# Between two transformer blocks: one pass over the residual for two norms, and the context normalised by token

## Chip, cores and metric

One Trainium2 chip, one core of it. The metric is the device time of one execution in microseconds (us), the median of several runs. All data are float32. Five engines work side by side: TensorE (PE in the profile; its weight loads are PEld), VectorE (DVE), ScalarE (ACT), GpSimd (POOL) and SyncE (SP), and 16 DMA engines move the data.

## What is computed

Two transformer blocks on 256 tokens of width 1024, one after the other. The first ends in a mixture of experts and a final norm, the second begins with a norm of its own and with a context of 256 more tokens. Cut to what lies between the blocks:

```python
# end of the first block
x = x + g2 * hier_moe(h, ...)                 # 32 experts, 2 for each token
x = rms_norm(x, final_g)
# start of the second block
h     = rmsnorm(x,   g_pre_mix) * (1 + sc1)      + sh1
h_ctx = rmsnorm(ctx, g_pre_mix) * (1 + mod_c[1]) + mod_c[0]
# ... then h @ w_in and h_ctx @ w_in[:, :KV_COLS], attention, merge,
x = x + gt1 * rmsnorm(y, g_post_mix)          # the residual x is used again
# ... then a second mixture of 32 experts, 4 for each token
```

`rms_norm(x, g)` is `x * rsqrt(mean(x*x) + 1e-6) * g`, the mean over the 1024 features.

## The kernel before

Activations lie transposed, features on the partitions: `xT` (the residual) and `hT` (the normalised input) hold 8 slices `k` of 128 features. `xT[:, k, :]` is 256 tokens wide. `hT[:, k, 0:T]` holds the tokens of `x` and `hT[:, k, T:2*T]` those of the context. A per-feature factor is thus one number for each partition, a per-token factor a row of 256 that is the same on all partitions. `hN` is a buffer with tokens on the partitions, and `mgd` is another view of the same memory. `gain[:, j, :]` holds products of gains, `mod2` the second block's shifts and scales, `cols` the gain vectors (`cols[:, 0, 64:72]` is `final_g`).

A norm goes so. ACT squares all 8 slices in one instruction (`square`, L1351). PE sums the squares over the features by 8 products with a matrix of ones (`sumsq`). DVE scales the sum and adds epsilon (`rms`, L1733), ACT takes the root (`sqrt`, L1348), DVE the reciprocal (L1735). DVE then multiplies each slice by gain and row (`modulate`, L1741) and, where there is a shift, adds it in a second loop (L1745). Each step waits for the one before by a semaphore; `mark` and `nth` count them.

Between the blocks three norms stand one after another: `fin` (the final norm, in place on `xT`), `n2` (the second block's norm of it, into `hT[:, :, 0:T]`) and `ctx` (the context's, into `hT[:, :, T:2*T]`). The context is fetched into `hN` by a DMA that POOL issues once the residual of the first block is made ("moe1 out"). PE transposes it in 16 blocks, ACT copies it out of PSUM and squares it. Only when all of "h2" and "hctx" is there does PE begin the projections (`fill2`).

Before that come the experts of the first block (`moe(1)`): 8 groups of 4 experts, whose weights (three chunks of 4 MB for a group) stream through a ring of 12 slots of 1 MB that SP fills. A slot is loaded again when PE has used it. Each engine walks its own program of this loop. The projections of the second block take their weights from the same ring, as do, later, the 32 experts of the second block (12 MB each).

POOL also fetches the attention biases (32 small DMAs, L548), the first 16 right behind the context. DVE, after the norms, normalises and rotates the heads that the first four fills give ("rope") and adds a mask to the biases (`bias(0)`, L1899).

Of the kernel before, what the change touches and what calls it, by code (L numbers as in the profile page):

```python
# [15 lines left out]
ALU = mybir.AluOpType  # L16
# [3 lines left out]
P = 128  # L20
# [119 lines left out]
class Counts:  # L140
# [13 lines left out]
    def nth(self, sem, key):  # L154

        return 1 if self.known is None else self.known[self.names[id(sem)], key]

def program(nc, A, const, ssm, tables, out, known):
# [3 lines left out]
    with ExitStack() as ctx:  # L163
# [104 lines left out]
        PT = [LA(1024), LA(1024)]  # L268
        sgl = LA(2, 2, T)
        mgd = hN[:, :, :].rearrange("p a b -> p (a b)").rearrange("p (k t) -> p k t", t=T)  # L270
        yS = LA(4, T)
        oT = LA(KD, T)
        stat = sb("stat", [P, 2, 16])
# [251 lines left out]
        def _(g):  # L525
# [8 lines left out]
                                                   cols[:, 0, 72 + 16 * kv + c:73 + 16 * kv + c], None, ALU.add)  # L534
                last.then_inc(blocks_made, 1)

            g.wait_ge(madeV, nth(madeV, "moe1 out"))
            g.dma_start(hN[:, :, :], A["ctx_2"].rearrange("(a p) d -> p a d", p=P)).then_inc(ctx_in, 16)

            for tt in range(TT):  # L540
                if tt == 1:
                    g.wait_ge(filled, nth(filled, ("S", 2, 3)))
                for h in range(8):
                    for r in range(2):
                        row = 2 * tt + r
                        src = bass.AP(tensor=A["rpb_2"].tensor, offset=h * 465 + (7 - row) * 31 + 15 - 63,
                                      ap=[[1, 64], [31, 4], [1, 64]])
                        g.dma_start(nab2[64 * r:64 * r + 64, h, :].rearrange("p (a b) -> p a b", b=64), src).then_inc(bias_in[tt], 16)  # L548
# [12 lines left out]
        def _(pe):  # L561
# [6 lines left out]
            def transpose(dst, src):  # L568
                return nc.tensor.transpose(dst, src, ident[0:src.shape[0], 0:src.shape[0]])  # L569
# [636 lines left out]

            last = mm(ps[:, 0, 0:1], ones, csil[:, 0:1], start=True, stop=True)
            last.then_inc(filled, mark(filled, "moe1"))
            sumsq("fin", 0, hT[:, :, T:2 * T])

            sumsq("n2", 0, hT[:, :, T:2 * T])
            pe.wait_ge(ctx_in, 16)
            for tt in range(TT):
                for k in range(KD):
                    last = transpose(ps[:, 1 + tt * 2 + k // 4, (k % 4) * P:(k % 4 + 1) * P], hN[:, tt, k * P:(k + 1) * P])
            last.then_inc(filled, mark(filled, "ctx"))
            pe.wait_ge(madeA, nth(madeA, ("sq", "ctx")))
            for k in range(KD):
                last = mm(ps[:, 5, 0:T], ones, mgd[:, k, :], start=k == 0, stop=k == KD - 1)
            last.then_inc(filled, mark(filled, ("ss", "ctx")))  # L1220
            pe.wait_ge(madeV, nth(madeV, "h2"))
            pe.wait_ge(madeV, nth(madeV, "hctx"))

            turn2 = [0]

# [7 lines left out]
            def fill2(outs):  # L1233

                b, g = bank2()
                for o, lhs, rhs in outs:
                    for k in range(KD):
                        last = mm(o(b), lhs(k), rhs(k), start=k == 0, stop=k == KD - 1)
                last.then_inc(filled, mark(filled, ("p2", g)))

# [96 lines left out]
        def _(act_):  # L1337
# [309 lines left out]
            sigmoids("gates")  # L1647
            moe_front(1)
            moe(1)
            act_.wait_ge(madeV, nth(madeV, "moe1 out"))  # L1650
            square("fin", xT[:, :, :])
            sqrt("fin", rstd[:, 0:T])
            act_.wait_ge(madeV, nth(madeV, "x2"))
            square("n2", xT[:, :, :])
            sqrt("n2", rstd[:, 0:T])
            act_.wait_ge(filled, nth(filled, "ctx"))
            for tt in range(TT):
                for q in range(2):
                    last = copy(hT[:, 4 * q:4 * q + 4, T + tt * P:T + (tt + 1) * P], ps[:, 1 + tt * 2 + q, :].rearrange("p (k t) -> p k t", t=P))
            act_.drain()  # L1660
            a(mgd, hT[:, :, T:2 * T], ACT.Square).then_inc(madeA, mark(madeA, ("sq", "ctx")))
            sqrt("ctx", rstd[:, T:2 * T])
            turn2 = [0]

            def take2(fn):
# [53 lines left out]
        def _(v):  # L1719
# [43 lines left out]
            def step(ins):  # L1763
                v.drain()
# [192 lines left out]
            tt_(gain[:, 0, :], mod2[:, 40:48, 0], cols[:, 1, 72:80], ALU.mult)  # L1957
            v.drain()
            tt_(wr1, wr1, B(gain[:, 1, :], 36), ALU.mult)
            merge("branch", "gates", "mgd")  # L1960
            clear_tables(1)
            for c in range(4):
# [213 lines left out]

            moe_front(1)
            moe(1)
            v.wait_ge(filled, nth(filled, "moe1"))
            for k in range(KD):  # L2180
                last = stt(xT[:, k, :], ps[:, 4 + k // 2, (k % 2) * T:(k % 2 + 1) * T], mod1[:, 40 + k:41 + k], xT[:, k, :], ALU.mult, ALU.add)
            last.then_inc(madeV, mark(madeV, "moe1 out"))
            rms("fin", 0, rstd[:, 0:T])
            modulate(xT[:, :, :], xT[:, :, :], rstd[:, 0:T], cols[:, 0, 64:72], None, "x2")

            V.memset(crow[:, 3, 2:3], 0.0).then_inc(madeV, mark(madeV, ("shift", 2)))
            rms("n2", 0, rstd[:, 0:T])
            modulate(hT[:, :, 0:T], xT[:, :, :], rstd[:, 0:T], gain[:, 2, :], mod2[:, 0:8, 0], "h2")
            rms("ctx", 5, rstd[:, T:2 * T])
            modulate(hT[:, :, T:2 * T], hT[:, :, T:2 * T], rstd[:, T:2 * T], gain[:, 3, :], mod2[:, 0:8, 1], "hctx")  # L2190

            v.wait_ge(emptied, nth(emptied, ("p2", 3)))
            q3 = lambda x: x.rearrange("p t (h d) -> p (t h) d", d=HD)
# [91 lines left out]
```

## Time and profile before

| what | us |
| --- | --- |
| median of 3 runs | 2142.71 |
| lowest and highest run | 2140.18, 2146.76 |
| the profiled execution | 2141.7 |
| its span, first to last instruction | 2139.9 |
| PE busy in it | 1885.5 (88%) |
| DVE, ACT, POOL busy | 538.6, 385.6, 44.5 |
| mean granted PE clock | 0.947 |
| mean DMA rate | 293 GB/s |

### The profile page before, as it was taken

The numbers are of one execution on the slowest core, as the hardware profiler recorded it, in microseconds if no ns is written. First come the engines' busy times: TensorE is split into PE (matmuls) and PEld (weight loads), VectorE is DVE, ScalarE is ACT, GpSimd is POOL, SyncE is SP. The second block draws the span as 40 slices with busy tenths as digits, with TensorE's granted clock in tenths as the row PEclk, the third lists the DMA queues.
The fourth block names the chain that finished last, engine by engine and source line by source line (L and its number), as shares of the span: only waits on it lengthen the run. The fifth ranks groups of instructions, "written<-read, shape, count | busy, mean of one in ns | idle before, by whom it ended". The sixth has DMA issues, their size and how long they took to land.

```text
span 2139.9 us, 28358 instructions
## 1 busy us (share of the span) xinstructions
PE 1885.5 (88%) x10935; PEld 1070.9 (50%) x10938; DVE 538.6 (25%) x1231; ACT 385.6 (18%) x875; POOL 44.5 (2%) x107
## 2 busy tenths in 40 slices
PE   6999999976686779999988999888998999988895
PEld 4664678854444466677753443333333344333333
DVE  3675332121111223232421111111111111111112
ACT  3232452021110110243120111111110111110012
POOL 0030000000000200100000000000000000000000
PEclk9999899988888889899978999999998999999998
DMA  9969622319999712233342999999999599999993
GB/s 399 370 232 358 240 79 88 149 36 417 418 418 387 272 43 79 67 92 102 142 169 112 416 418 417 416 416 418 417 417 401 241 417 418 416 417 417 418 417 152
DMA packets 108344, 626.77 MB, mean 293 GB/s; under 512 B 11168, under 2 KB 15264, under 8 KB 49792
## 3 DMA queue, kind: packets, MB, share of 16 engines
q1 hardware_dynamic: 106112, 618.81, 71.5%
q0 software_dynamic: 1584, 4.33, 1.1%
q10 hardware_dynamic: 560, 2.35, 0.3%
q8 instruction: 70, 1.15, 0.2%
q14 instruction: 18, 0.15, 0.0%
HBM read 624.39 MB, written 1.05 MB: 292 GB/s over the span
## 4 chain that ended last, share of the span: by engine, by line
PE 59%; DMA 21%; SPq 11%; issue 3%; DVE 3%; ACT 2%; DVEq 0%; ACTq 0%
PE ps L452 56%; DMA ring<-in_w_gu_dram 14%; SPq L501 6%; SPq L504 5%; DMA ring<-in_moe_w_gate_dram 4%; PE ps L569 3%; DMA ring<-in_ada_w_dram 1%; ACT arena L1344 1%; DMA ring<-in_moe_w_down_dram 1%; DMA ring<-in_w_mod_dram 1%; SPq L474 0%; DVE rstd L1735 0%; DVE arena L2099 0%; PE ps L815 0%; SPq L411 0%
## 5 line engine op out<-in xcount | busy, mean ns | idle before, releaser
L452 PE MATMUL ps<-ring,arena 128*64 128x512 f32 (+2 forms) x5248 | 918.4, 564 | 126.7 <-issue 54.5
L452 PEld LDWEIGHTS ps<-ring,arena 128*64 128x64 f32 (+1 forms) x5248 | 293.5, 131 | 692.2 <-issue 501.5
L452 PE MATMUL ps<-arena 64*128 64x256 f32 (+10 forms) x1762 | 263.0, 378 | 31.9 <-ACT arena L1344 15.9
L452 PE MATMUL ps<-hT,ring 128*128 128x256 f32 (+1 forms) x960 | 237.0, 402 | 2.3 <-DVE hT L1781 2.3
L452 PEld LDWEIGHTS ps<-arena 64*128 64x128 f32 (+6 forms) x1764 | 155.6, 164 | 136.4 <-issue 76.4
L452 PEld LDWEIGHTS ps<-hT,ring 128*128 128x128 f32 x960 | 180.3, 192 | 58.8 <-issue 33.7
L2125 DVE TENSOR_SCALAR arena<-ps 128x512 f32<-128x512 f32 x34 | 23.5, 692 | 549.9 <-PE ps L452 549.9
L1344 ACT ACTIVATE arena<-ps 128x256 f32<-128x256 f32 (+4 forms) x195 | 107.3, 574 | 291.3 <-PE ps L452 150.3
L1608 ACT ACTIVATE arena<-ps,mod,gain 128x128 f32<-128x128 f32 x180 | 67.7, 458 | 435.2 <-PE ps L452 435.2
L452 PE MATMUL ps<-arena,hN 128*128 128x128 f32 (+1 forms) x960 | 129.0, 294 | 15.4 <-DVE arena L2075 9.0
L452 PEld LDWEIGHTS ps<-arena,hN 128*128 128x128 f32 x960 | 120.0, 205 | 40.8 <-issue 16.7
L1619 ACT ACTIVATE arena<-arena 128x512 f32<-128x512 f32 (+1 forms) x44 | 25.7, 584 | 615.9 <-DVE arena L2125 417.1
L452 PE MATMUL ps<-ring,hT 128*128 128x256 f32 (+2 forms) x416 | 82.7, 377 | 8.4 <-DVE hT L1745 8.4
L569 PE MATMUL ps<-consts,arena 128*128 128x128 f32 x526 | 75.0, 280 | 11.3 <-DVE arena L2131 8.2
L452 PEld LDWEIGHTS ps<-ring,hT 128*128 128x128 f32 (+1 forms) x416 | 70.1, 186 | 21.6 <-DVE hT L1745 8.8
L2113 DVE COPY arena<-ps 128x512 f32<-128x512 f32 x34 | 23.5, 692 | 220.0 <-PE ps L452 220.0
L452 PE MATMUL ps<-arena,ring 128*128 128x256 f32 x352 | 76.5, 380 | 0.7 <-ACT arena L1344 0.7
L569 PEld LDWEIGHTS ps<-consts,arena 128*128 128x128 f32 x526 | 61.4, 143 | 28.9 <-DVE arena L2131 10.5
L452 PEld LDWEIGHTS ps<-arena,ring 128*128 128x128 f32 x352 | 66.7, 190 | 10.3 <-ACT arena L1344 0.9
L1517 ACT ACTIVATE arena<-ps,stat 128x15 f32<-128x15 f32 (+3 forms) x128 | 56.1, 448 | 80.8 <-DVE stat L1877 80.8
L1877 DVE TENSOR_REDUCE stat<-ps 128x2 f32<-128x1024 f32 (+3 forms) x40 | 36.7, 917 | 131.2 <-PE ps L452 131.2
L452 PE MATMUL ps<-hN,ring 128*128 128x256 f32 x256 | 56.4, 380 | 0.0
(257 smaller groups left out, 920.1 us busy)
## 6 DMA issues: line engine op xcount, KB each, us to landing
ring<-in_w_gu_dram SPq DMA_DIRECT2D x256, 1024.0 KB, 20.0
ring<-in_w_dn_dram SPq DMA_DIRECT2D x128, 1024.0 KB, 23.3
ring<-dense_dram SPq DMA_DIRECT2D x56, 1024.0 KB, 10.6
ring<-in_moe_w_gate_dram SPq DMA_DIRECT2D x32, 1024.0 KB, 12.7
ring<-in_moe_w_up_dram SPq DMA_DIRECT2D x32, 1024.0 KB, 19.1
ring<-in_moe_w_down_dram SPq DMA_DIRECT2D x32, 1024.0 KB, 18.1
ring<-in_ada_w_dram SPq DMA_DIRECT2D x24, 1024.0 KB, 18.3
ring<-in_w_mod_dram SPq DMA_DIRECT2D x24, 1024.0 KB, 8.6
```

The lines of the kernel that those rows point to most:

```text
L452: ins = nc.tensor.matmul(*a, start=start, stop=stop, **k)
L501: sp.dma_start(ring[:, i % RING, :], src).then_inc(full[i % RING], 16)
L504: sp.dma_start(slot_ap(i, (2, D)), src).then_inc(full[i % RING], 16)
L569: return nc.tensor.transpose(dst, src, ident[0:src.shape[0], 0:src.shape[0]])
L1344: return a(dst, src, ACT.Copy, scale=scale)
L1517: last = a(e_[:, s * nk:s * nk + m], ps[:, bank, at:at + m], ACT.Exp, bias=stat[:, i % 2, s:s + 1], accum_out=stat[:, i % 2, 4 + s:5 + s])
L1608: last = a(dst[:, d, :], ps[:, bank, k * P:(k + 1) * P], ACT.Identity, scale=gs[:, d:d + 1], bias=sh[:, d:d + 1])
L1619: a(sg[:, 0:w], glu[:, 0:w], ACT.Sigmoid, scale=1.702 if n == 2 else 1.0).then_inc(s["sig"], 1)
L1877: V.tensor_reduce(dst, sc[:, :, :, 0:m], AX.X, ALU.max, negate=True).then_inc(madeV, mark(madeV, ("mx", n, i)))
L2113: V.tensor_copy(dst, ps[:, 3, :]).then_inc(s["ys"], 1)
L2125: ts(glu, ps[:, 1, :], 7.0, None, ALU.min).then_inc(s["glu"], 1)
```

## The change

- The residual is made in four chunks of two slices ("moe1 out", c). For each chunk ACT writes two sets of squares: of `x` into `mgd` and of `x * final_g` into `o2`. PE sums both, into two banks.
- The two norms are merged. With s1 = mean(x*x) and s2 = mean((x*final_g)^2), DVE forms s2 + eps*(s1 + eps). One over its root is the product of both norms' rows. `gain[:, 2, :]` gets `final_g` as a further factor, and `hT[:, :, 0:T]` is made from `xT` directly. DVE multiplies, ACT adds the shift, chunk by chunk, and the first fill waits for each chunk as it comes to it.
- The residual itself is scaled by `final_g` and its own row afterwards.
- The context is fetched after "router" of the first block, into `ctxN`, a view of memory in `hT` that is free then. Its statistics are taken with tokens on the partitions, by ACT with `accum_out`, in ACT's program behind its loop of the experts. PE transposes the rows already scaled (`context_turn`), and ACT applies gain and shift as it copies them out of PSUM (`context_out`). PE no longer sums squares of the context.
- POOL's first 16 bias DMAs wait for "moe1" instead of "moe1 out".

```diff
+        hflat = hT[:, :, :].rearrange("p a b -> p (a b)")
+        ctxN = hflat[:, 0:TT * D].rearrange("p (a b) -> p a b", b=D)
 # POOL
-            g.wait_ge(madeV, nth(madeV, "moe1 out"))
-            g.dma_start(hN[:, :, :], A["ctx_2"].rearrange("(a p) d -> p a d", p=P)).then_inc(ctx_in, 16)
+            g.wait_ge(filled, nth(filled, ("router", 1)))
+            g.dma_start(ctxN, A["ctx_2"].rearrange("(a p) d -> p a d", p=P)).then_inc(ctx_in, 16)
+            g.wait_ge(filled, nth(filled, "moe1"))
 # PE
-            sumsq("fin", 0, hT[:, :, T:2 * T])
-            sumsq("n2", 0, hT[:, :, T:2 * T])
-            pe.wait_ge(ctx_in, 16)
-            for tt in range(TT):
+            def context_turn(tt, bank):
                 for k in range(KD):
-                    last = transpose(ps[:, 1 + tt * 2 + k // 4, (k % 4) * P:(k % 4 + 1) * P], hN[:, tt, k * P:(k + 1) * P])
-            last.then_inc(filled, mark(filled, "ctx"))
-            pe.wait_ge(madeA, nth(madeA, ("sq", "ctx")))
-            for k in range(KD):
-                last = mm(ps[:, 5, 0:T], ones, mgd[:, k, :], start=k == 0, stop=k == KD - 1)
-            last.then_inc(filled, mark(filled, ("ss", "ctx")))
-            pe.wait_ge(madeV, nth(madeV, "h2"))
-            pe.wait_ge(madeV, nth(madeV, "hctx"))
+                    last = transpose(ps[:, bank + k // 4, (k % 4) * P:(k % 4 + 1) * P], ctxN[:, tt, k * P:(k + 1) * P])
+                last.then_inc(filled, mark(filled, ("ctx", tt)))
+            pe.wait_ge(madeA, nth(madeA, "ctx rows"))
+            context_turn(0, 2)
+            for c in range(4):
+                pe.wait_ge(madeA, nth(madeA, ("sq", "fin", c)))
+                for k in (2 * c, 2 * c + 1):
+                    for n, sq in enumerate((mgd, o2)):
+                        last = mm(ps[:, n, 0:T], ones, sq[:, k, :], start=k == 0, stop=k == KD - 1)
+                if c == 1:
+                    context_turn(1, 4)
+            last.then_inc(filled, mark(filled, ("ss", "fin")))
 # PE, fill2
+                if g == 1:
+                    pe.wait_ge(madeA, nth(madeA, "hctx"))
                 for o, lhs, rhs in outs:
                     for k in range(KD):
+                        if g == 0 and k % 2 == 0:
+                            pe.wait_ge(madeA, nth(madeA, ("h2", k // 2)))
 # ACT
-            square("fin", xT[:, :, :])
+            act_.wait_ge(ctx_in, 16)
+            for tt in range(TT):
+                a(hflat[:, (2 + tt) * D:(3 + tt) * D], ctxN[:, tt, :], ACT.Square, accum_out=rn[:, tt:tt + 1])
+            act_.drain()
+            a(rn[:, 4:6], rn[:, 0:2], ACT.Sqrt, scale=1.0 / D, bias=rn[:, 2:3]).then_inc(madeA, mark(madeA, "ctx std"))
+            act_.wait_ge(madeV, nth(madeV, "ctx r"))
+            for tt in range(TT):
+                last = a(ctxN[:, tt, :], ctxN[:, tt, :], ACT.Identity, scale=rn[:, 4 + tt:5 + tt])
+            last.then_inc(madeA, mark(madeA, "ctx rows"))
+            for c in range(4):
+                act_.wait_ge(madeV, nth(madeV, ("moe1 out", c)))
+                a(mgd[:, 2 * c:2 * c + 2, :], xT[:, 2 * c:2 * c + 2, :], ACT.Square)
+                for k in (2 * c, 2 * c + 1):
+                    last = a(o2[:, k, :], xT[:, k, :], ACT.Square, scale=cols[:, 0, 64 + k:65 + k])
+                last.then_inc(madeA, mark(madeA, ("sq", "fin", c)))
+            def context_out(tt, bank, ks):
+                for k in ks:
+                    last = a(hT[:, k, T + tt * P:T + (tt + 1) * P], ps[:, bank + k // 4, (k % 4) * P:(k % 4 + 1) * P], ACT.Identity,
+                             scale=gain[:, 3, k:k + 1], bias=mod2[:, k, 1:2])
+                return last
+            act_.wait_ge(filled, nth(filled, ("ctx", 0)))
+            context_out(0, 2, (0, 1, 4, 5, 6, 7))
             sqrt("fin", rstd[:, 0:T])
-            act_.wait_ge(madeV, nth(madeV, "x2"))
-            square("n2", xT[:, :, :])
-            sqrt("n2", rstd[:, 0:T])
-            act_.wait_ge(filled, nth(filled, "ctx"))
-            for tt in range(TT):
-                for q in range(2):
-                    last = copy(hT[:, 4 * q:4 * q + 4, T + tt * P:T + (tt + 1) * P], ps[:, 1 + tt * 2 + q, :].rearrange("p (k t) -> p k t", t=P))
-            act_.drain()
-            a(mgd, hT[:, :, T:2 * T], ACT.Square).then_inc(madeA, mark(madeA, ("sq", "ctx")))
-            sqrt("ctx", rstd[:, T:2 * T])
+            act_.wait_ge(filled, nth(filled, ("ctx", 1)))
+            context_out(0, 2, (2, 3))
+            context_out(1, 4, range(KD)).then_inc(madeA, mark(madeA, "hctx"))
+            for c in range(4):
+                act_.wait_ge(madeV, nth(madeV, ("h2 scaled", c)))
+                for k in (2 * c, 2 * c + 1):
+                    last = a(hT[:, k, 0:T], hT[:, k, 0:T], ACT.Identity, bias=mod2[:, k, 0:1])
+                last.then_inc(madeA, mark(madeA, ("h2", c)))
+            sqrt("x2", rstd[:, T:2 * T])
 # DVE, with the other gains of the first block
+            tt_(gain[:, 2, :], gain[:, 2, :], cols[:, 0, 64:72], ALU.mult)
+            V.memset(rn[:, 2:3], EPS)
 # DVE, between the blocks
+            v.wait_ge(madeA, nth(madeA, "ctx std"))
+            V.reciprocal(rn[:, 4:6], rn[:, 4:6]).then_inc(madeV, mark(madeV, "ctx r"))
             v.wait_ge(filled, nth(filled, "moe1"))
+            for c in range(4):
+                for k in (2 * c, 2 * c + 1):
+                    last = stt(xT[:, k, :], ps[:, 4 + k // 2, (k % 2) * T:(k % 2 + 1) * T], mod1[:, 40 + k:41 + k], xT[:, k, :], ALU.mult, ALU.add)
+                last.then_inc(madeV, mark(madeV, ("moe1 out", c)))
+            V.memset(crow[:, 3, 2:3], 0.0).then_inc(madeV, mark(madeV, ("shift", 2)))
+            v.wait_ge(filled, nth(filled, ("ss", "fin")))
+            r12, r1 = rstd[:, 0:T], rstd[:, T:2 * T]
+            step(ts(r12, ps[:, 0, 0:T], EPS / D, EPS * EPS, ALU.mult, ALU.add))
+            stt(r12, ps[:, 1, 0:T], 1.0 / D, r12, ALU.mult, ALU.add).then_inc(madeV, mark(madeV, ("var", "fin")))
+            ts(r1, ps[:, 0, 0:T], 1.0 / D, EPS, ALU.mult, ALU.add).then_inc(madeV, mark(madeV, ("var", "x2")))
+            v.wait_ge(madeA, nth(madeA, ("std", "fin")))
+            step(V.reciprocal(r12, r12))
+            for c in range(4):
+                for k in (2 * c, 2 * c + 1):
+                    last = stt(hT[:, k, 0:T], xT[:, k, :], gain[:, 2, k:k + 1], r12, ALU.mult, ALU.mult)
+                last.then_inc(madeV, mark(madeV, ("h2 scaled", c)))
+            v.wait_ge(madeA, nth(madeA, ("std", "x2")))
+            step(V.reciprocal(r1, r1))
             for k in range(KD):
-                last = stt(xT[:, k, :], ps[:, 4 + k // 2, (k % 2) * T:(k % 2 + 1) * T], mod1[:, 40 + k:41 + k], xT[:, k, :], ALU.mult, ALU.add)
-            last.then_inc(madeV, mark(madeV, "moe1 out"))
-            rms("fin", 0, rstd[:, 0:T])
-            modulate(xT[:, :, :], xT[:, :, :], rstd[:, 0:T], cols[:, 0, 64:72], None, "x2")
-            V.memset(crow[:, 3, 2:3], 0.0).then_inc(madeV, mark(madeV, ("shift", 2)))
-            rms("n2", 0, rstd[:, 0:T])
-            modulate(hT[:, :, 0:T], xT[:, :, :], rstd[:, 0:T], gain[:, 2, :], mod2[:, 0:8, 0], "h2")
-            rms("ctx", 5, rstd[:, T:2 * T])
-            modulate(hT[:, :, T:2 * T], hT[:, :, T:2 * T], rstd[:, T:2 * T], gain[:, 3, :], mod2[:, 0:8, 1], "hctx")
+                stt(xT[:, k, :], xT[:, k, :], cols[:, 0, 64 + k:65 + k], r1, ALU.mult, ALU.mult)
```

## Rows read from the trace of the kernel before

**Rows 1.** The page, part 4: the chain that ended last, by engine.
```profile
PE 59%; DMA 21%; SPq 11%; issue 3%; DVE 3%; ACT 2%; DVEq 0%; ACTq 0%
```
**Rows 2.** The chain in order of time: start us, us, what.
```profile
725.38 0.69 DVE arena L2111
...
774.93 98.28 PE ps L452 x384
...
1290.96 25.20 DMA ring<-in_w_gu_dram
```
**Rows 3.** Timeline between the blocks: start, us, engine, line, what [idle before <-releaser].
```profile
718.67 0.67 ACT L1344 ACTIVATE arena<-ps 128x256 f32<-128x256 f32 x2
...
726.12 3.72 PE L452 MATMUL ps<-arena 128*128 128x256 f32 x16 [1.41 <-DVE arena L2111]
...
729.99 3.23 DVE L2181 SCALAR_TENSOR_TENSOR xT<-ps,mod,xT 128x256 f32<-128x256 f32 x8 [3.93 <-PE ps L452]
...
735.18 1.28 ACT L1348 ACT_TABLE_LOAD   x1
...
735.21 6.28 PE L452 MATMUL ps<-hT,consts 128*128 128x256 f32 x16 [5.26 <-ACT hT L1351]
741.53 0.43 DVE L1733 TENSOR_SCALAR rstd<-ps 128x256 f32<-128x256 f32 x1 [8.31 <-PE ps L452]
741.99 0.42 ACT L1348 ACTIVATE rstd<-rstd 128x256 f32<-128x256 f32 x1 [5.53 <-DVE rstd L1733]
742.44 1.75 DVE L1735 RECIPROCAL rstd<-rstd 128x256 f32<-128x256 f32 x1 [0.48 <-ACT rstd L1348]
744.27 3.26 DVE L1741 SCALAR_TENSOR_TENSOR xT<-xT,cols,rstd 128x256 f32<-128x256 f32 x8
...
755.32 1.91 PE L569 MATMUL ps<-consts,hN 128*128 128x128 f32 x16
...
772.64 2.19 DVE L1745 TENSOR_SCALAR hT<-hT,mod 128x256 f32<-128x256 f32 x8
```
**Rows 4.** Windows of 2 us: stretch, busy us by engine, PEclk, DMA share, GB/s.
```profile
730.00:732.00 2.00, 0.00 (x0) 0.00 (x0) 2.00 (x6) 0.00 (x0) 0.00 (x0) 1.00 0.98 406
732.00:734.00 2.00, 0.00 (x0) 0.00 (x0) 1.22 (x4) 0.75 (x1) 0.47 (x1) 0.90 1.05 438
734.00:736.00 2.00, 0.79 (x2) 0.70 (x3) 0.00 (x0) 1.98 (x2) 2.00 (x4) 0.50 1.00 414
...
756.00:758.00 2.00, 1.23 (x12) 0.99 (x10) 1.57 (x1) 1.13 (x3) 0.00 (x0) 1.00 0.00 0
...
774.00:776.00 2.00, 1.07 (x3) 0.92 (x4) 0.83 (x4) 0.00 (x0) 0.00 (x0) 0.50 0.00 0
```
**Rows 5.** Windows during the first experts, same columns.
```profile
440.00:460.00 20.00, 12.38 (x152) 10.53 (x156) 5.40 (x19) 4.89 (x9) 0.00 (x0) 0.83 0.01 2
...
520.00:560.00 40.00, 24.35 (x256) 15.04 (x260) 5.02 (x12) 2.47 (x7) 0.00 (x0) 0.79 1.01 417
```
**Rows 6.** ACT by form, whole span: busy us, mean ns of one, idle before.
```profile
L1608 ACT ACTIVATE arena<-ps,mod,gain 128x128 f32<-128x128 f32 x180 | 67.7, 458 | 435.2 <-PE ps L452 435.2
...
L1517 ACT ACTIVATION_READ_ACCUMULATOR arena<-ps,stat 128x1 f32 x128 | 25.7, 201 | 0.0
L1344 ACT ACTIVATE arena<-ps 128x1024 f32<-128x1024 f32 x24 | 24.6, 1025 | 29.6 <-PE ps L569 29.5
...
L1583 ACT ACTIVATE hT<-xT 128x512 f32<-128x512 f32 x8 | 5.0, 630 | 72.4 <-DVE xT L1966 66.8 <-DVE xT L2244 5.6
...
L1700 ACT ACTIVATE arena<-ps,gain 128x256 f32<-128x256 f32 x8 | 3.4, 470 | 48.3 <-PE ps L452 48.3
```
**Rows 7.** Timeline of the projections: head rotation on DVE, end of the fills.
```profile
808.84 2.29 DVE L1899 TENSOR_TENSOR arena<-arena,consts 128x2048 f32<-128x2048 f32 x1
...
821.85 0.29 DVE L2219 COPY arena<-arena 128x256 f32<-128x256 f32 x1
...
873.04 1.91 PE L569 MATMUL ps<-consts,arena 128*128 128x128 f32 x16
```

More of the change, by code:

```diff
@@ L1649, in _ @@
             moe(1)
-            act_.wait_ge(madeV, nth(madeV, "moe1 out"))
-            square("fin", xT[:, :, :])
-            sqrt("fin", rstd[:, 0:T])
-            act_.wait_ge(madeV, nth(madeV, "x2"))
-            square("n2", xT[:, :, :])
-            sqrt("n2", rstd[:, 0:T])
-            act_.wait_ge(filled, nth(filled, "ctx"))
-            for tt in range(TT):
-                for q in range(2):
-                    last = copy(hT[:, 4 * q:4 * q + 4, T + tt * P:T + (tt + 1) * P], ps[:, 1 + tt * 2 + q, :].rearrange("p (k t) -> p k t", t=P))
```

## The prediction, made before the changed kernel was run

> **What bounds the kernel now.** First I read the page's chain: 59% of it is PE, 21% DMA, and DVE and ACT together only 5% [rows 1]. So work on DVE or ACT counts only where PE stands and waits for it. Then the chain in order of time around the change: the last copy of the experts' output on DVE at 725.38, and one unbroken piece of 98.28 us of PE from 774.93, the projections [rows 2]. The timeline between these two shows what lies there. DVE makes the residual from 729.99 [rows 3]. From then to 774.93 the engines hand one another a chain with nothing beside it: squares, sums, root, reciprocal, multiply, three times over. That is 44.9 us, of which PE needs little. All of it is on the path that sets the end, and this is the stretch the change rebuilds.
>
> Behind it the chain is PE up to the second experts and then DMA [rows 2]. Their weights stream through a ring whose slots PE frees, so an earlier start of PE is an earlier start of everything. I count a microsecond won at 774.93 as a microsecond at the end.
>
> **Part 1, the context's load.** It moves to the point where the first block's router is done. In a window soon after it the DMA engines are busy 0.01 of the time, while they are full at 417 GB/s from 520 on [rows 5]. If the 1 MB lands in the idle stretch it costs nothing; if it falls entirely into the full one it costs 1.05 MB / 417 GB/s = 2.5 us. The idle stretch is nearer: I take 0. POOL issues nothing else in between, so the new wait holds back only its bias loads, which come some microseconds earlier than before.
>
> **Part 2, the context's rows.** They lie in ACT's program behind its loop, so they run at the tail of the last group and not during the first experts. ACT's last copy there ends at 719.34 (718.67 + 0.67 [rows 3]). Then come two squares of 1024 elements with a sum each, at 1.03 + 0.20 us [rows 6] = 2.5; the table load that stood at 735.18, 1.28 us [rows 3]; and a small root, 0.3. With half a microsecond to leave the loop that ends at about 723.9. DVE is busy with the last copy until 726.07 (725.38 + 0.69 [rows 2]), so it does the reciprocal at once, and ACT scales the rows, 2 x 1.1 us, to 728.6. PE's sums of the experts' output run to about 729.9 [rows 3]. The cover is 1.3 us. Without it, whatever ACT is late delays PE's first transposes and ACT's first squares; all of Part 2 uncovered would be 6.5 us.
>
> **Part 3, the sums.** DVE makes the residual in 3.23 us, 0.81 for a chunk of two slices [rows 3]: chunk 0 at 730.9, the others at 731.6, 732.4, 733.2. ACT needs for each chunk a square of 512 elements and two of 256 with a scale from memory. The first I take at 0.57, a bit under the mean of 0.63 for one, since neighbours overlap; the second is 3.4 / 8 = 0.42 [rows 6]. That is 1.43 for a chunk, so ACT gives chunk 0 at 732.4 and chunk 3 at 736.6. PE needs four products of 256 columns for a chunk. The scatter just before gives 3.72 / 8 = 0.465 us for one at full clock; the sums of the old norm took 6.28 / 8 = 0.785 [rows 3], for which the clock was at 0.50 when they began [rows 4]. I take full clock: PE is busy to 729.9 in both kernels, the new sums begin 2.5 us later, and in the old kernel the clock still read 1.00 and 0.90 in the windows from 730 to 734 with PE idle [rows 4]. So each chunk is 1.86 us and PE, not ACT, sets the pace. Four chunks are 7.4 us, and the second half of the context's transposes stands among them, 8 x 0.12 = 1.0 us by the 1.91 us for sixteen [rows 3]. The sums end at 732.4 + 8.4 = 740.8.
>
> Here a rule speaks against the full clock. The Trainium skill ("TensorE: Matmul & The Clock Gate", Part 4: PE-mode transpose) says that transposes do not count as activity for the clock in the way products do. The eight transposes at about 730 would then keep nothing awake, and those in the middle would be a gap. The trace does not bear it out plainly: in the window from 756 to 758, which holds the end of the sixteen transposes, the clock was 1.00 [rows 4]. By the rule taken strictly the sums would run as in the second rival below.
>
> **Part 4, from the sums to PE.** DVE forms the variance in two dependent steps of 0.43 [rows 3], with a drain 1.0 us: 741.8. ACT's root is 0.42: 742.3. DVE's reciprocal is 1.75, its first chunk 0.82 (3.26 for eight [rows 3]): 744.9. ACT meanwhile has ten pieces of the context to write out, each of 128 elements with scale and bias from memory. One alone is 0.46 [rows 6], in a row I take 0.38, so 3.8 us: 746.1. The first six were done while PE summed. Then ACT adds the shift to chunk 0, 2 x 0.42: PE starts at 747.0. So ACT, not DVE, is late here, by 1.2 us. Later chunks come every 0.85 us. PE begins at half clock, as it did at 774 [rows 4], and needs 1.57 us for two slices, so it doesn't wait for them. The context is complete before fill 1 wants it. At 0.46 for each piece, and 0.53 for each add, the start would be 748.0.
>
> On this the Trainium skill ("ScalarE: Activation LUTs", Rules for kernel authors) says that adds and multiplies belong on VectorE. The trace agrees: DVE's shift is 2.19 / 8 = 0.27 us [rows 3] against 0.42 here. By the rule the two adds would follow DVE's own multiply and PE would start at about 745.6; as built, 747.0.
>
> **What is removed** is the rest: two of the three roots and reciprocals on the path, the second and third sum, and 16 multiplies and 16 adds in whole loops. None of it needs a price of its own, because I compare start with start: 774.93 - 747.0 = 27.9 us.
>
> **Part 5, what moves behind.** The residual's own reciprocal and eight multiplies (1.75 + 3.26 [rows 3]) now follow on DVE, beside the first fills. DVE then finds fills 0 to 3 to rotate. That work ended at 822.14 while PE came for it at 873.04 [rows 7]: 51 us of cover, of which nothing is used, as both move. The biases were in by 808.84 [rows 7]; they are wanted 28 us earlier now and issued 4 us earlier. They share that cover. The one more gain on DVE lies before the first experts, where it waits for PE: 0 to 0.2 us. Extra waits in the first fill: 0 to 0.5 us.
>
> **The sum.** The profiled execution took 2141.7 us (its span 2139.9 and 1.8 around it); 2141.7 - 27.9 + 0.3 = 2114.1. It lay 1.0 below the median of the runs shown, so against that I expect 2115; I predict 2114.5.
>
> **Rivals.**
> First, a late ACT. Its program behind the loop starts late, or its pieces don't overlap. For it: three of my prices are from rows of other shapes, and the cover in Part 2 is 1.3 us. Against: before, ACT had nothing to do from 719.34 until the residual was made [rows 3]. Price 1 to 6.5 us: 2115.5 to 2121, middle 2118.
> Second, sums at half clock. Sixteen products at 0.785 are 12.6 us instead of 7.4, and the transposes 2.0 instead of 1.0: + 6.2, so 2120.7. For it: PE does only 1 us of transposes between 729.9 and 732.4. Against: [rows 4] as above.
> Third, the gain is given back before the end: the biases or the rotation turn up late for the attention. It would need more than the 51 us of cover to be gone. That would be no change, 2142. I see no mechanism in the rows.
> Fourth, on the other side: slower. The new first fill begins with a wait at each of its pairs of slices. If this keeps the clock at 0.50 in the projections, their 98.28 us [rows 2], nearly all at full clock, would double at worst: 2114 + 90 = 2204. It decides from 34 us more, about a third of the projections at half clock. Against: chunks come at 0.85 us and PE uses 1.57 for each at half clock, so it has no gaps.
>
> **How the numbers follow.** The forecast, 2110 to 2117, gets 0.62. A late ACT gets 0.20, half clock 0.11, the third 0.02, the fourth 0.02, and 0.03 is for a gain over 32 us, if ACT's pieces are cheaper and the chain shorter than priced. From the forecast's lower end to the half-clock case with the load's 2.5 us is 2109 to 2123, about 0.9; I keep it, since the bounds ask for it. Less than 0.3% (6.4 us) is about what a measurement of this kernel can't tell from no change. Faster by more: 0.95; within: 0.03; slower: 0.02.
>
> **What would show it.** In the profile after: ACT's squares of the rows ended before 724 and its scaled rows before 730; PE's sums with "ones" from 732.4 to 740.8 in about 7.4 us busy at a clock of 1.00; ACT's context pieces between 742.3 and 746; the first product of hT at 747, and the same 98 us behind it; no new wait of PE up to the first scores. The prediction is wrong if the projections start after 751, if the stretch up to 726 grows because the load met the experts' weights, or if what was won at 747 isn't there at the end.

## The result, and the profile after

The changed kernel takes 2108.26 us (median of 4 runs, 2107.66 to 2109.01), the kernel before in the same comparison 2141.44. The ratio is 0.9844, with a 95% interval of 0.9831 to 0.9858: 33.2 us less. I had predicted 2114.5 with a range of 2109 to 2123, so the sign and the mechanism held and the gain was larger than the range allowed. The measured median lies 0.7 us below the range.

The timeline of the changed kernel between the blocks, start, us, engine, line, what:

```profile
716.85 0.67 ACT L1353 ACTIVATE arena<-ps 128x256 f32<-128x256 f32 x2
...
719.64 1.28 ACT L1663 ACT_TABLE_LOAD   x1
...
720.94 0.30 ACT L1663 ACTIVATE rn<-rn 128x2 f32<-128x2 f32 x1
...
724.35 2.19 ACT L1666 ACTIVATE hT<-hT,rn 128x1024 f32<-128x1024 f32 x2 [3.12 <-DVE rn L2213]
...
728.17 3.23 DVE L2217 SCALAR_TENSOR_TENSOR xT<-ps,mod,xT 128x256 f32<-128x256 f32 x8 [3.86 <-PE ps L454]
...
729.09 0.63 ACT L1670 ACTIVATE hN<-xT 128x512 f32<-128x512 f32 x1 [2.54 <-DVE xT L2217]
...
730.56 0.70 PE L454 MATMUL ps<-hN,consts 128*128 128x256 f32 x2 [1.50 <-ACT arena L1672]
...
734.12 1.04 PE L572 MATMUL ps<-consts,hT 128*128 128x128 f32 x8
...
738.02 0.59 PE L454 MATMUL ps<-arena,consts 128*128 128x256 f32 x2
738.65 0.42 DVE L2223 TENSOR_SCALAR rstd<-ps 128x256 f32<-128x256 f32 x1 [7.24 <-PE ps L454]
...
739.62 0.42 ACT L1357 ACTIVATE rstd<-rstd 128x256 f32<-128x256 f32 x1 [3.08 <-DVE rstd L2224]
739.94 3.59 ACT L1678 ACTIVATE hT<-ps,mod,gain 128x128 f32<-128x128 f32 x10
740.07 1.75 DVE L2227 RECIPROCAL rstd<-rstd 128x256 f32<-128x256 f32 x1 [0.15 <-ACT rstd L1357]
741.89 3.25 DVE L2230 SCALAR_TENSOR_TENSOR hT<-xT,gain,rstd 128x256 f32<-128x256 f32 x8
743.37 3.32 ACT L1691 ACTIVATE hT<-hT,mod 128x256 f32<-128x256 f32 x8
...
744.46 30.04 PE L454 MATMUL ps<-ring,hT 128*128 128x256 f32 x128 [5.85 <-ACT hT L1691]
```

Read it against [rows 3]. From the start of the residual to the first projection there were 44.94 us, now there are 16.29 (744.46 - 728.17). The context's root was done at 721.24, and its scaled rows at 726.54, before PE had summed the experts' output. PE's sums, with the transposes among them, run without a gap from 730.56 to 738.61. ACT's ten pieces of the context end at 743.53, and the first shift waits for them: DVE's first chunk was ready at 742.77.

The windows show the clock. A row has the stretch, its length, the busy times of PE, PEld, DVE, ACT and POOL, and then the granted share, here 1.00, 1.00, 0.80 and 0.50:

```profile
730.00:734.00 4.00, 3.44 (x16) 3.05 (x17) 1.41 (x5) 4.00 (x11) 4.00 (x8) 1.00 1.05 312
734.00:738.60 4.60, 4.60 (x26) 3.77 (x24) 0.00 (x0) 2.54 (x8) 4.26 (x7) 1.00 1.03 224
738.60:744.40 5.80, 0.01 (x1) 0.00 (x0) 5.44 (x11) 4.78 (x14) 0.00 (x0) 0.80 0.99 266
744.40:748.00 3.60, 3.54 (x8) 2.87 (x9) 1.72 (x3) 2.60 (x7) 0.00 (x0) 0.50 0.93 248
```

The sums ran at 1.00 throughout. The clock fell while PE stood for 5.8 us, and the projections began at 0.50.

To see where the 33 us come from I cut four profiles at the same five events: two executions of the kernel before and two of the changed one. The events are the start of the residual (R), the first projection (F), the first scores of the second block's attention (S), the merge behind the attention (M, a piece of 57.26 us on the chain), and the second experts in their steady pace (B, the piece of 20.2 us). The last column is the span of the profile. Worked out from timeline and chain:

| us | to R | R to F | F to S | S to M | M to B | B to end | span |
| --- | --- | --- | --- | --- | --- | --- | --- |
| before | 729.99 | 44.94 | 102.48 | 125.51 | 164.32 | 972.7 | 2139.9 |
| before, second profile | 730.97 | 45.01 | 102.49 | 125.52 | 164.33 | 972.6 | 2140.9 |
| changed | 728.17 | 16.29 | 103.16 | 123.20 | 162.71 | 973.7 | 2107.2 |
| changed, second profile | 729.40 | 16.28 | 102.95 | 123.18 | 159.46 | 973.5 | 2104.8 |
| mean difference | -1.7 | -28.7 | +0.6 | -2.3 | -3.2 | +1.0 | -34.4 |

The stretch that I costed gives 28.7. The rest, 5.7 us in these profiles, is spread over places that the change doesn't touch. The experiments ask whether it depends on when the projections start, on one part of the change, or on something else.

### The profile page after: what moved, and what is told of

Its sections match the earlier page's. It is cut to its first block, busy times and chain, and to the rows that moved or that the text cites. A ratio compares the mean times of both kernels' runs of the same rounds, so it can differ in the third digit from the quotient of the medians.

```text
span 2107.2 us, 28339 instructions
## 1 busy us (share of the span) xinstructions
PE 1873.6 (89%) x10921; PEld 1062.7 (50%) x10922; DVE 528.8 (25%) x1209; ACT 396.0 (19%) x910; POOL 44.4 (2%) x107
## 4 chain that ended last, share of the span: by engine, by line
PE 59%; DMA 22%; SPq 11%; issue 3%; DVE 2%; ACT 2%; DVEq 1%; ACTq 0%
PE ps L454 57%; DMA ring<-in_w_gu_dram 14%; SPq L503 5%; SPq L506 5%; DMA ring<-in_moe_w_gate_dram 4%; PE ps L572 3%; DMA ring<-in_ada_w_dram 1%; ACT arena L1353 1%; DMA ring<-in_moe_w_down_dram 1%; DMA ring<-in_w_mod_dram 1%; SPq L476 0%; DVE arena L2132 0%; PE ps L818 0%; DVEq L1795 0%; ACT arena L1617 0%
```

## The experiments

Each kernel is the changed one with a small edit, unless it says otherwise. Ratios are to the kernel before on the same chip, with their 95% interval.

**1. A delay put back.** Seventeen idle reciprocals on DVE give the projections nearly their old place.

```diff
+            for n in range(17):
+                V.reciprocal(mgd[:, n % 8, :], cst("time", 1, T + 1))
+                if n % 8 == 7:
+                    v.drain()
             step(V.reciprocal(r12, r12))
```

> The changed kernel with 17 reciprocals of 256 elements on DVE put ahead of its own (they write to memory that nobody reads; the output is unchanged). They delay the first projection by 17 x 1.75 less the 0.6 us by which ACT was later than DVE, 29.3 us, which puts it 45.6 us behind the residual where the kernel before had 44.9. Theory 'one for one': only the start of the projections counts, and the 4.5 us that the change won beyond its stretch of 28.7 us are scatter or lie elsewhere in the change; then 2108.3 + 29.3 = 2137.6, ratio to before 0.998. Rival 'everything hangs on the start' (a later start also lands later pieces worse, so all of the 33.2 goes): 2142, ratio 1.000. Rival 'absorbed': under 2130.

Measured: 2136.17 us, ratio 0.9981 (0.9972 to 0.9989). R to F is 43.50 (729.35 to 772.85), 27.2 more than in the changed kernel, and the total is 27.9 more than 2108.3. One for one holds within the noise: the two kernels ran in different comparisons, and by their ratios to the kernel before the difference is 29 us. The rival that ties everything to the start falls: with a stretch only 1.5 us shorter than before, the kernel is still 3.8 us faster than the 2140.0 measured beside it.

**2. The norms alone.** The context goes the old way; its sums stand between the first and the second fill.

```diff
-            g.wait_ge(filled, nth(filled, ("router", 1)))
-            g.dma_start(ctxN, ...)
+            g.wait_ge(madeV, nth(madeV, ("moe1 out", 3)))
+            g.dma_start(hN[:, :, :], ...)
 ...
                 if g == 1:
-                    pe.wait_ge(madeA, nth(madeA, "hctx"))
+                    pe.wait_ge(madeA, nth(madeA, ("sq", "ctx")))
+                    for k in range(KD):
+                        last = mm(ps[:, 6, 0:T], ones, mgd[:, k, :], start=k == 0, stop=k == KD - 1)
+                    last.then_inc(filled, mark(filled, ("ss", "ctx")))
+                    pe.wait_ge(madeV, nth(madeV, "hctx"))
```

> The merged, chunked norms alone; the context is loaded when the residual is made and goes the old way (turned, copied, squared, summed, scaled on DVE), its sums between the first and the second fill. PE waits for the load before its transposes, until about 746 instead of 744.5, starts fill 0 at 749, then stands before fill 1 for squares, sums and scaling of the context until about 768 where the changed kernel was there at 752. One for one: 2108.3 + 16.6 = 2125, ratio 0.992. Rival: the context's part hides beside fill 0 and the norms alone give nearly all: 2112, ratio 0.986.

Measured: 2127.46 us, ratio 0.9940 (0.9927 to 0.9953). The timeline has the waits that were expected, first for the load and then for the scaled context:

```profile
746.96 3.67 PE L571 MATMUL ps<-consts,hN 128*128 128x128 f32 x16 [5.47 <-DMA hN<-in_ctx_dram]
750.43 7.33 PE L454 MATMUL ps<-ring,hT 128*128 128x256 f32 x32
757.59 3.62 PE L454 MATMUL ps<-hN,consts 128*128 128x256 f32 x16
769.56 20.77 PE L454 MATMUL ps<-ring,hT 128*128 128x256 f32 x83 [8.35 <-DVE hT L1768]
```

The norms alone leave the context's chain bare. It hid nothing but its load beside them. The total is 2.5 us above the 2125 expected, and the chain of this run has an idle time of PE of 2.33 us before the second experts, which the changed kernel lacks (experiment 6).

**3. The context's part alone.** The norms run one after another as before, with their squares in `mgd`. The edit is shown against the kernel before.

```diff
+            sumsq("fin", 0, mgd)
+            context_turn(1, 4)
+            sumsq("n2", 0, mgd)
+            pe.wait_ge(madeV, nth(madeV, "h2"))
+            pe.wait_ge(madeA, nth(madeA, "hctx"))
```

> The context's part alone; the two norms run one after another in the old way, with their squares in another buffer. The old chain had h2 33.8 us behind the start of the residual and the context's chain took 11.1 us more. One for one counted from the changed kernel (16.3 us): 2108.3 + 17.5 = 2125.8, ratio 0.993. Counted from the kernel before: 2141.4 - 11.1 = 2130.3, ratio 0.995. Which of the two it is tells whether the 4.5 us that are not in the stretch belong to the norms or to the context's load and rows.

Measured: 2124.52 us, ratio 0.9928 (0.9915 to 0.9941). R to F is 34.03 (729.29 to 763.32). Counted from the changed kernel, 17.7 us more in the stretch make 16.3 in the total, within 1.3 of the expectation. Counted from before, 10.9 us less in the stretch make 15.5. So this kernel has the extra gain, without the merged norms.

**4. The load at a bad time.** POOL waits for two groups of experts.

```diff
-            g.wait_ge(filled, nth(filled, ("router", 1)))
+            g.wait_ge(S[1, "first"]["down"], 2)
```

> The changed kernel with the context's load held back until two groups of experts are done, so that its 1 MB falls into the stretch where the DMA engines are full. By DMA time 1.05 MB / 417 GB/s = 2.5 us: the last residual 2.5 us later and 2110.8, ratio to before 0.9856. Rival: the ring has slack there and it costs nothing: 2108.3, ratio 0.9845.

Measured: 2113.21 us, ratio 0.9871 (0.9857 to 0.9886), 5 us more than the changed kernel. The load is issued at 519.03 into full DMA engines and takes 13.2 us to land, where it took 5.5 in the idle stretch. The residual starts at 733.38; in ten profiles with the early load it starts between 728.2 and 731.6 (mean 729.5). My 2.5 us for the worst case were too low: in this one profile the load costs 3.9 us at R, more than the time its bytes take, though the ten others scatter over 3.4 us. Why it is more stays open. As built, no cost of the load can be seen.

**5. The kernel before, once more.**

> The kernel before, unchanged, for a second profile. The first one showed two things behind the projections that the changed kernel lacked: 2.4 us more from the first scores to the merge, where the granted clock read 0.50 for longer, and an idle time of PE of 2.1 us in front of the first weights of the second experts. If they belong to the program they come again at the same places; if they are scatter of one execution they don't. Expected: the idle time comes again (it is also in the run with the norms alone, whose context part is the old one), the low clock doesn't.

Measured: 2141.64 us, ratio 1.000 (0.9991 to 1.0010). I expected one of the two oddities to come again; both did. S to M is 125.52 us as in the first profile, because the clock stays low for longer. The second pair of products that add the mask to the scores takes 2.07 us in this run and in the first profile:

```profile
881.43 2.07 PE L452 MATMUL ps<-arena,consts 128*128 128x256 f32 x4
```

In both profiles of the changed kernel it takes 1.13:

```profile
851.38 1.13 PE L454 MATMUL ps<-arena,consts 128*128 128x256 f32 x4
```

The granted share over the first 7.5 us or so of the scores was 0.58 in the kernel before (877.4 to 885.0) and 0.77 in the changed one (847.6 to 855.0). The idle time of PE is there too, in the chain of this run (start, us, what):

```profile
1096.40 1.03 PE ps L452 x4
1097.43 2.15 issue
1099.58 5.48 PE ps L452 x15
```

So both belong to the program and are not scatter. The changed kernel, run again beside it, took 2108.06 us, ratio 0.9845 (0.9832 to 0.9859). Its expectation was:

> The changed kernel, unchanged, as the control for what runs beside it. 2108.3, ratio 0.985.

**6. Eight products more on PE.**

```diff
             last.then_inc(filled, mark(filled, ("ss", "fin")))
+            for k in range(8):
+                mm(ps[:, 7, 0:T], ones, mgd[:, k % 8, :], start=k == 0, stop=k == 7)
```

> The changed kernel with eight more products with ones on PE behind the last sum, into a bank that nobody reads, where PE is idle for 5.9 us (the output is unchanged). They take 3.5 us, so PE stands for 2.4 us before the projections, and the clock should be 1.00 when these begin: the first 3 us of them at full clock save 1.5. They also make the program of PE as long as before. Theory 'place of the code': the 2.1 us of idle PE in front of the second experts come when the instructions lie as before, so they come back here and the sum is 2108.3 - 1.5 + 2.1 = 2108.9. Rival: that idle time has nothing to do with PE's instructions, 2106.8.

Measured: 2109.37 us, ratio 0.9854 (0.9839 to 0.9869). The idle time is back, in the same place as in the kernel before:

```profile
1062.90 1.03 PE ps L454 x4
1063.93 2.37 issue
1066.30 4.09 PE ps L454 x9
```

In the changed kernel the same spot has none:

```profile
1062.39 0.63 issue
1063.03 7.38 PE ps L454 x16
```

The four products ahead of the idle time add the experts' biases. The total, 1.3 us above the changed kernel beside it, can't show the idle time: the intervals overlap. The other half of the expectation was mis-sized. F to S shrank by 0.5 us, not by 1.5: after 2.39 us without a product the clock read 0.64 in the first 3.4 us of the projections.

**7. Twelve products more.** The same edit with 12.

> As the run with eight more products on PE, but with twelve. Theory 'place of the code': the idle time of 2.1 to 2.4 us before the second experts' first weights depends on where PE's instructions lie, so with four products more it is gone or sits elsewhere. Rival 'length': any program of PE that is as long as before or longer has it, and it is there again. PE is idle 0.7 us instead of 2.4 before the projections, so these begin at 1.00 and save 1.5 us against the changed kernel, where the eight saved 0.5.

Measured: 2109.40 us, ratio 0.9856 (0.9841 to 0.9871). The idle time has moved. It now lies ahead of the four bias products, where the other kernels have 0.63 to 0.66 us, and is longer, 3.64 us:

```profile
1061.86 0.44 ACT arena L1619
1062.30 3.64 issue
1065.93 2.77 PE ps L454 x7
```

PE's straight-line code between the blocks has 40 products and transposes in the kernel before, in the norms alone and with eight more: idle 2.1 to 2.4 us behind the bias products. With 44 it is 3.0 us ahead of them. With 32 (the changed kernel, the context's part alone, the delay and the rest) there is none. "It moves with the code" holds in all these runs. The part of the expectation on the clock held as well: with a gap of 0.67 us the projections began at 1.00 and F to S took 100.98 us, 2.2 less than in the changed kernel. S to M was 1.6 us shorter as well, 121.52, with a granted share of 1.00 where the scores begin (848.8 to 856.0). The total shows none of this: 3.0 us of it went into the idle time, and the residual of the profiled execution started late, at 731.58.

**8. ACT's pieces ahead of its root.**

```diff
-            sqrt("fin", rstd[:, 0:T])
             act_.wait_ge(filled, nth(filled, ("ctx", 1)))
             context_out(0, 2, (2, 3))
-            context_out(1, 4, range(KD)).then_inc(madeA, mark(madeA, "hctx"))
+            context_out(1, 4, range(6))
+            sqrt("fin", rstd[:, 0:T])
+            context_out(1, 4, (6, 7)).then_inc(madeA, mark(madeA, "hctx"))
```

> The changed kernel with eight of the ten last pieces of the context on ACT ahead of its root, in the 3.1 us in which it waits for the sums. If ACT's pieces set the start of the projections, it moves from 16.3 to 15.5 us behind the residual: 2107.5, ratio to the changed kernel 0.9996. Rival: the root is held up by as much as is won, no change in the stretch.

Measured: R to F 15.69 us (730.28 to 745.97), 0.6 less, so ACT's pieces did set the start. The total, 2110.19 us with a ratio of 0.9850 (0.9836 to 0.9864), can't show 0.6 us and doesn't.

**9. No chunks.** All waits are for the last chunk.

```diff
-                act_.wait_ge(madeV, nth(madeV, ("moe1 out", c)))
+                act_.wait_ge(madeV, nth(madeV, ("moe1 out", 3)))
-                pe.wait_ge(madeA, nth(madeA, ("sq", "fin", c)))
+                pe.wait_ge(madeA, nth(madeA, ("sq", "fin", 3)))
-                act_.wait_ge(madeV, nth(madeV, ("h2 scaled", c)))
+                act_.wait_ge(madeV, nth(madeV, ("h2 scaled", 3)))
-                            pe.wait_ge(madeA, nth(madeA, ("h2", k // 2)))
+                            pe.wait_ge(madeA, nth(madeA, ("h2", 3)))
```

> The changed kernel with every chunk's wait set to the last chunk: ACT squares once the whole residual is made, PE sums once all squares are there, the shift and the projections likewise. Same instructions, no overlap. One after another: residual 3.2, squares 5.3, sums with the second half of the transposes 7.8, variance to reciprocal 3.3, eight multiplies 3.3, eight adds 3.4 and gaps: 26.6 us behind the start of the residual instead of 16.3, so 2118.4, ratio 0.9895. Rival: PE's clock falls while it waits for the squares, then 3 to 5 us more, 2122.

Measured: 2121.36 us, ratio 0.9911 (0.9897 to 0.9924). R to F is 29.30 us. The rival with the clock decides it. PE stands for 7.79 us before the squares are there, and the sums begin at half speed:

```profile
738.93 1.22 PE L454 MATMUL ps<-hN,consts 128*128 128x256 f32 x2 [7.79 <-ACT arena L1672]
...
739.95 1.06 PE L454 MATMUL ps<-arena,consts 128*128 128x256 f32 x2
...
744.62 0.59 PE L454 MATMUL ps<-arena,consts 128*128 128x256 f32 x2
```

The sums and transposes take 10.6 us (738.93 to 749.55) where they take 8.1 in the changed kernel. The chunks are worth 13 us, about 2.5 of them because PE never waits long enough to lose its clock.

**10. The transposes behind the sums.** The second half of the context is turned while PE would stand, and ACT writes the last four pieces out behind the shifts. DVE waits for the transposes before it writes over their source, which costs nothing: they end at 738.80, and its first multiply starts at 741.20.

```diff
-                if c == 1:
-                    context_turn(1, 4)
             last.then_inc(filled, mark(filled, ("ss", "fin")))
+            context_turn(1, 4)
 ...
             act_.wait_ge(filled, nth(filled, ("ctx", 1)))
             context_out(0, 2, (2, 3))
-            context_out(1, 4, range(KD)).then_inc(madeA, mark(madeA, "hctx"))
+            context_out(1, 4, range(4))
 ...  # behind the shifts, ahead of sqrt("x2")
+            context_out(1, 4, range(4, KD)).then_inc(madeA, mark(madeA, "hctx"))
 ...
             step(V.reciprocal(r12, r12))
+            v.wait_ge(filled, nth(filled, ("ctx", 1)))
```

> The changed kernel with the second half of the context's transposes behind the last sum instead of between the sums, and with only six pieces of the context on ACT between the root and the first shift; the last four follow the shifts. The sums end 0.87 us earlier, and ACT is ready when DVE's first chunk is: the projections start 14.7 us behind the residual instead of 16.3. PE's program is as long as the changed kernel's, so the idle time before the second experts stays away. 2108.1 - 1.6 = 2106.5, ratio to before 0.9838. Rival: the won 1.6 us don't show in the total, whose runs scatter by 3 us.

Measured: 2104.91 us, ratio 0.9835 (0.9819 to 0.9851). R to F is 14.81 us, as expected:

```profile
737.76 1.04 PE L572 MATMUL ps<-consts,hT 128*128 128x128 f32 x8
...
742.11 3.30 ACT L1690 ACTIVATE hT<-hT,mod 128x256 f32<-128x256 f32 x8 [0.69 <-DVE hT L2231]
...
743.17 7.09 PE L454 MATMUL ps<-ring,hT 128*128 128x256 f32 x18 [4.37 <-ACT hT L1690]
```

Now it is DVE that ACT's shift waits for. This is the fastest version: clearly faster than the kernel before, and 3 us under the changed kernel in the median, but the two ratios' intervals overlap. Only the 1.5 us in the stretch are shown: behind it F to S took 0.8 us more and S to M 1.6 us less than in the changed kernel.

**11. The shift on DVE.** ACT's loop of adds is gone, and PE waits for DVE's chunks.

```diff
                 for k in (2 * c, 2 * c + 1):
                     stt(hT[:, k, 0:T], xT[:, k, :], gain[:, 2, k:k + 1], r12, ALU.mult, ALU.mult)
+                v.drain()
+                for k in (2 * c, 2 * c + 1):
+                    last = ts(hT[:, k, 0:T], hT[:, k, 0:T], mod2[:, k, 0:1], None, ALU.add)
```

> The changed kernel with the shift added by DVE behind its own multiply, chunk by chunk, instead of ACT. DVE needs 0.27 us for an add where ACT needs 0.41, and doesn't wait for ACT's ten pieces: the first chunk is ready 15.3 us behind the residual instead of 16.3. 2107.1. Rival: DVE's multiply and add of all chunks, 5.9 us in a row, come too slowly for PE, and the first fill stands; no gain.

Measured: R to F 15.44 us (729.60 to 745.04), 0.85 less. F to S is 103.61, 0.45 more, and the total 2109.20 us with a ratio of 0.9855 (0.9840 to 0.9870): no gain that can be measured.

## Why the prediction was right, and where it was wrong

**Place of the gain: right.** The stretch between the residual and the first projection was the place, and its work was the predicted one. Predicted 17.0 us, measured 16.29 and 16.28. Part by part, counted from the start of the residual:

| step | predicted | measured |
| --- | --- | --- |
| context's root done (before it) | 6.1 | 6.9 |
| context's rows done (before it) | 1.4 | 1.6 |
| sums begin | 2.4 | 2.39 |
| sums end | 10.8 | 10.44 |
| DVE's first chunk | 14.9 | 14.60 |
| ACT free of the context | 16.1 | 15.36 |
| first projection | 17.0 | 16.29 |

The sums took 8.1 us for my 8.4. ACT's ten pieces took 3.6 for my 3.8, and started 0.5 us earlier. All errors are of one sign and small; together they are 0.7 us. Chunking was worth 13 us (experiment 9).

**First rival, a late ACT: no.** The cover in Part 2 was there, and ACT left its loop at once, without my half microsecond.

**Second rival, sums at half clock: no, and its mechanism is real.** The products ran at 1.00. The eight transposes at 728.00 and the 1.5 us without work behind them didn't cost the clock. Where PE stood for 7.79 us, in experiment 9, it did, and the sums took 2.5 us more. My 6.2 was too high, because the clock came back inside the sums. The rule on transposes (the Trainium skill, "TensorE: Matmul & The Clock Gate", Part 4: PE-mode transpose) cost nothing here. The window from 728.00 to 730.00, which holds the first eight, read 1.00, and so did the one from 734.00 to 738.60 with the other eight. No run here shows transposes letting the clock fall; in the changed kernel they stand next to products every time, so the rule isn't refuted either.

**Third rival, given back: no; it had 51 us of cover, and nothing came late. Fourth rival, half clock in the projections: no.** The clock read 0.50 from 744.40 to 748.00 and 0.89 from 748.00 to 752.00, and F to S was 103.16 us against 102.48.

**The rule that adds belong on VectorE** (the Trainium skill, "ScalarE: Activation LUTs", Rules for kernel authors) agrees with the stretch: with DVE adding, F came 0.85 us earlier (experiment 11), where I had worked out 1.4. No gain showed in the total. F to S took 0.45 us more, and the clock read 0.70 from 748 to 752, where the changed kernel had 0.89; why it came back later wasn't tested. What made ACT late was less the adds than the ten pieces queued ahead of them: without those, F came 0.6 us earlier (experiment 8).

**The step that failed** is in the part on what bounds the kernel: "I count a microsecond won at 774.93 as a microsecond at the end". As a rule for the time won there it holds: 27.2 us put back gave 27.9 (experiment 1), 13.0 gave 13.1 (experiment 9), by the ratios 29 and 14. But it was taken to mean that nothing else changes behind F, and two things did. With the kernel before, PE has an idle time of 2.1 us in front of the second experts' first weights, and the scores' first products run longer at half clock, 2.3 us. Both came in both profiles of the kernel before and in neither of the changed one. The first follows the number of products and transposes on PE between the blocks (experiments 2, 5, 6, 7); the change takes 8 of them away. I had priced removed products by their time between the blocks alone. Not all of the 2.1 us arrives: M to B is 164.3 to 164.9 us in the five profiles with the idle time, 162.7 to 163.2 in six of the nine without it, and 159.4 to 161.8 in the other three, the second profile of the changed kernel among them. So the idle time is worth about 1.5 us, and the rest of the table's -3.2 is the clock in that one profile (1.00 in the 10 us from the loop's start, 0.83 in the first profile).

The second is not settled. Its 2.3 us are absent from every other kernel here, the norms alone and the context's part alone too, whose S to M is 123.11. S to M takes three lengths: 125.5 in both profiles of the kernel before, 121.5 in experiments 7 and 10, and 123.1 to 123.2 in all others. It goes with the granted clock over the first scores. In their first 7 to 8 us that was 0.58 in the kernel before, 0.77 in the changed one and 1.00 in experiment 7. Experiment 10 had 0.76 there, and then 1.00 from 854 to 860 where the changed kernel had 0.81 from 855 to 860. What sets that clock wasn't tested.

The table's -1.7 us before R isn't shown to be the change's. Ten profiles with the early load have R between 728.2 and 731.6, three with the old one between 730.0 and 731.0. The scatter is as large as the difference.

**The range** failed by 0.7 us, with the idle time and the scores' clock, 4.4 us in the profiles, outside every term. From my 2114.5 to the measured 2108.3 are 6.2 us: 0.7 from the stretch, 2.3 from the scores' clock, about 1.5 from the idle time. The remaining 1.7 have no cause that the runs show; the medians of the kernel before alone lie between 2140.0 and 2141.6 in the comparisons here. The range reached 8.5 us on the side of the rivals and 5.5 on the other, and its lower end, 2109, has no term of its own: the forecast ended at 2110. I had given a gain over 32 us a chance of 0.03, for cheaper pieces on ACT. The gain came out so large, but those pieces gave 0.2 us of it.

**The load:** no cost to be seen, as predicted, but the bound for the bad case, 2.5 us by bytes over rate, was too low: the one profile of experiment 4 shows 3.9.

## What to carry to other kernels

When a serial chain of square, sum, root and scale stands between two stages, cut it into chunks so that PE is fed from the first one: besides the overlap, PE then kept its clock here (1.00 against 0.50 at the start of the sums in experiment 9). On the engine that runs latest, put work that nobody waits for yet (here ACT's ten pieces) behind what the next stage waits for. Here a gain in the stretch that bounds the kernel arrived whole at the end, within 2 us. Still compare whole profiles by stage afterwards. Here 2 to 3 us came or went at distant places, with the length of PE's code or with the clock there.

## What the runs showed of the hardware

PE stood without a wait that the profile shows, and that depended on the code before it. With 40 or more products and transposes in the straight-line code between the blocks, it stood 2.1 to 3.0 us where the second experts' loop starts, and the spot moved with four products more. The queue for instructions is active just ahead of the gap in the kernel before (1095.8 to 1096.4, gap from 1096.39) and inside it with twelve products more (at 1063.5, gap from 1062.30). But the changed kernel, which has no gap, shows packets of that queue too, at 1063.5 to 1063.9, just behind the loop's first products at 1063.03. I take the idle time for code that comes late; that cause is only argued, and only the dependence on the code's length is shown.

A 1 MB load from POOL landed in 5.5 us with idle DMA engines and in 13.2 with full ones, and the residual that waits behind the weights' stream started 3.9 us later in that profile, where the bytes are worth 2.5.
